# x tiles requested first on the sync queue, small parameters on the other queues, squares of tiles 1 and 3 on VectorE: a hybrid decoder block on one core

## What is computed

```python
h    = rmsnorm(x, attn_norm_w)            # x * rsqrt(mean(x*x) + eps) * w
proj = h @ w_in                           # 1024 x 3080: q, k, v, z, beta, a, conformer
qkv  = silu(causal_dwconv(proj[q,k,v], gdn_conv_w))
o    = chunked_gated_delta_rule(l2norm(q), l2norm(k), v, g, beta)   # 4 heads, chunks of 64
u    = silu(layernorm(causal_dwconv(glu(proj[cf]), cf_dw_w) + cf_dw_b, cf_ln_w, cf_ln_b))
x    = x + concat(gated_rmsnorm(o, z), u) @ w_out
x    = x + moe(rmsnorm(x, ffn_norm_w))    # top 4 of 32 experts, clamped SwiGLU
out  = rmsnorm(x, final_norm_w)
```

## Time and profile before

| | us |
|---|---|
| median of 3 runs | 1394.98 |
| lowest, highest | 1392.49, 1396.18 |
| span of the profiled execution | 1395.8 |
| first projection matmul (L1797) starts | 20.09 |
| TensorE busy | 1241.0 (89%) |
| VectorE, GpSimd, ScalarE busy | 679.5, 320.3, 223.3 |

### The profile page before, as it was taken

How to read it: one execution, slowest core, us unless ns; L and a number is a source line. 1 busy time by engine, 2 the same in 40 slices (tenths; PEclk the granted TensorE clock), 3 DMA queues, 4 the chain that set the end, 5 groups by cost and what they waited for, 6 DMA issues and landing times.

```text
span 1395.8 us, 32044 instructions
## 1 busy us (share of the span) xinstructions
PE 1241.0 (89%) x12814; PEld 585.9 (42%) x12815; DVE 679.5 (49%) x1360; ACT 223.3 (16%) x439; POOL 320.3 (23%) x432
## 2 busy tenths in 40 slices
PE   6999999999599999899899999798978887879992
PEld 3444454564235554353534445233432332335331
DVE  2898885444644364335434433345443334353428
ACT  3125543412100011000000100000110000001103
POOL 5001111000322224222223212222233222222221
PEclk9999999999799999999999999999999999999996
DMA  9212000312589999999999999999999999999996
GB/s 307 85 61 91 1 31 1 142 74 86 210 337 400 409 418 424 425 426 426 426 425 425 424 426 425 426 426 425 426 424 425 426 427 425 426 426 426 380 407 245
DMA packets 59374, 455.33 MB, mean 326 GB/s; under 512 B 13308, under 2 KB 23604, under 8 KB 34214
## 3 DMA queue, kind: packets, MB, share of 16 engines
q1 hardware_dynamic: 44262, 432.59, 74.8%
q0 software_dynamic: 11568, 18.92, 3.7%
q10 hardware_dynamic: 3504, 3.26, 0.9%
HBM read 445.02 MB, written 14.81 MB: 329 GB/s over the span
## 4 chain that ended last, share of the span: by engine, by line
PE 58%; DMA 29%; DVE 7%; issue 2%; ACT 2%; ACTq 1%; POOL 0%; SPq 0%; DVEq 0%; POOLq 0%
PE bank L2136 26%; DMA ring<-in_w_gate_up_dram 15%; PE bank L2189 14%; DMA dslots<-in_w_down_dram 14%; PE bank L1797 6%; PE bank L1987 4%; DVE dslots L1122 3%; PE bank L1792 2%; DVE hbuf L1697 1%; PE bank L1865 1%; PE bank L1872 1%; PE bank L2100 1%; PE bank L2122 1%; PE bank L1952 1%; PE bank L1956 1%
## 5 line engine op out<-in xcount | busy, mean ns | idle before, releaser
L2136 PE MATMUL bank<-ring,wq 128*32 128x512 f32 x4992 | 566.6, 601 | 64.9 <-DMA ring<-in_w_gate_up_dram 56.2
L2136 PEld LDWEIGHTS bank<-ring,wq 128*32 128x32 f32 x4992 | 208.8, 111 | 381.1 <-issue 344.3
L2189 PE MATMUL bank<-dslots,intra 128*32 128x256 f32 x5056 | 284.7, 380 | 22.6 <-DMA dslots<-in_w_down_dram 21.8
L2189 PEld LDWEIGHTS bank<-dslots,intra 128*32 128x32 f32 x5056 | 169.1, 110 | 148.3 <-issue 54.6
L1510 DVE TENSOR_REDUCE small<-bank 128x4 f32<-128x8 f32 x33 | 5.5, 166 | 409.8 <-PE bank L2100 409.8
L1007 ACT ACTIVATE zrows<-intra 128x1024 f32<-128x1024 f32 x31 | 32.8, 1059 | 790.0 <-DVE intra L1603 763.8
L1797 PE MATMUL bank<-hbuf,ring 128*128 128x512 f32 x320 | 148.5, 604 | 0.7 <-ACT hbuf L748 0.7
L616 POOL COPY idx_in<-idx 128x4 int32 (+1 forms) x32 | 11.8, 370 | 555.6 <-DVE wq L1488 534.4
L1575 DVE STREAM_TRANSPOSE wq<-bank 128x512 f32<-128x512 f32 x124 | 77.8, 685 | 71.7 <-PE bank L2136 71.7
L621 POOL DMA_INDIRECT wq<-xn_rows,idx_in x82 | 100.5, 1225 | 44.3 <-POOL idx_in L616 28.0
L626 POOL DMA_INDIRECT y_rows<-rows,idx_out x79 | 81.0, 1025 | 52.5 <-POOL idx_out L616 25.2
(11 more groups left out here) (294 smaller groups left out, 894.4 us busy)
## 6 DMA issues: line engine op xcount, KB each, us to landing
ring<-in_w_gate_up_dram SPq DMA_DIRECT2D x127, 2048.0 KB
dslots<-in_w_down_dram SPq DMA_DIRECT2D x61, 2048.0 KB
ring<-in_w_in_dram SPq DMA_DIRECT2D x12, 1024.0 KB, 13.5
ring<-in_w_out_dram SPq DMA_DIRECT2D x4, 1024.0 KB, 5.6
ring<-in_w_down_dram SPq DMA_DIRECT2D x4, 1024.0 KB
dslots<-y_rows SPq DMA_DIRECT2D x2, 2048.0 KB, 20.1
hbuf<-in_x_dram SPq DMA_DIRECT2D x4, 512.0 KB, 5.4
dslots<-in_w_down_dram SPq DMA_DIRECT2D x2, 1024.0 KB, 4.7
```

Source lines behind the costliest of these rows:

```text
L2136: ins = M(bank[g][GROUP * j:GROUP * (j + 1), :], x[:, g, c * GROUP:(c + 1) * GROUP], w[:, :, j * QD:(j + 1) * QD], start=(c == 0), stop=(c ...
L2189: ins = M(b[GROUP * j:GROUP * (j + 1), col:col + QD], actT[:, g, c * GROUP:(c + 1) * GROUP], w[:, cc, j * QD:(j + 1) * QD], start=(c == 0 ...
```

## The change

All four x tiles are requested by SyncE, ahead of everything else on its queue. The six small parameter tensors move to ScalarE's queue, behind cf_dw_w. The three gate requests move to GpSimd, behind the identity and before the masks. normcol moves on ScalarE's queue behind the four tiles. The squares of tiles 1 and 3 move to VectorE (a scalar_tensor_tensor with accumulated sum), which signals ScalarE by a new semaphore, `ssx_ready`; ScalarE keeps Ln and Exp of all tiles.

```diff
@@ block.sync
-            sp.dma_start(xr[:, 0, :], x2d[0:P, :]).then_inc(x_in[0], 16)
-            for i, v in enumerate((cf_dw_b, cf_ln_w, cf_ln_b)):
-                sp.dma_start(prow[TAPS + i:TAPS + i + 1, :], v).then_inc(param_in, 16)
-            sp.dma_start(prow[34:46, :], gdn_conv_w[0].rearrange("w (s c) -> (w s) c", s=3)).then_inc(param_in, 16)
-            sp.dma_start(prow[46:48, :], attn_norm_w.rearrange("o (r c) -> (o r) c", r=2)).then_inc(param_in, 16)
-            sp.dma_start(prow[48:50, :], ffn_norm_w.rearrange("o (r c) -> (o r) c", r=2)).then_inc(param_in, 16)
+            for t in range(T):
+                sp.dma_start(xr[:, t, :], x2d[t * P:(t + 1) * P, :]).then_inc(x_in[t], 16)
             for u in range(NU):
@@ block.gpsimd
             pool.wait_ge(consts_ready, 1)
+            pool.dma_start(wab, win[:, :, OFF_BA:OFF_BA + 2 * H]).then_inc(gate_in, 16)
+            pool.dma_start(dtb, gdn_dt_bias[0:1, :].to_broadcast([P, H])).then_inc(gate_in, 16)
+            pool.dma_start(nA, gdn_a_log[0:1, :].to_broadcast([P, H])).then_inc(gate_in, 16)
@@ block.scalar
             act.dma_start(prow[0:TAPS, :], cf_dw_w[0]).then_inc(param_in, 16)
-            for t in range(1, T):
-                act.dma_start(xr[:, t, :], x2d[t * P:(t + 1) * P, :]).then_inc(x_in[t], 16)
-            act.dma_start(wab, win[:, :, OFF_BA:OFF_BA + 2 * H]).then_inc(gate_in, 16)
-            act.dma_start(dtb, gdn_dt_bias[0:1, :].to_broadcast([P, H])).then_inc(gate_in, 16)
-            act.dma_start(nA, gdn_a_log[0:1, :].to_broadcast([P, H])).then_inc(gate_in, 16)
-            act.dma_start(normcol, gdn_norm_w.rearrange("o p -> p o")).then_inc(late_in, 16)
+            for i, v in enumerate((cf_dw_b, cf_ln_w, cf_ln_b)):
+                act.dma_start(prow[TAPS + i:TAPS + i + 1, :], v).then_inc(param_in, 16)
+            act.dma_start(prow[34:46, :], gdn_conv_w[0].rearrange("w (s c) -> (w s) c", s=3)).then_inc(param_in, 16)
+            act.dma_start(prow[46:48, :], attn_norm_w.rearrange("o (r c) -> (o r) c", r=2)).then_inc(param_in, 16)
+            act.dma_start(prow[48:50, :], ffn_norm_w.rearrange("o (r c) -> (o r) c", r=2)).then_inc(param_in, 16)
             act.wait_ge(consts_ready, 1)
             for t in range(T):
                 act.wait_ge(x_in[t], 16)
-                own.mark(A(zrows[:, (t % 2) * D:(t % 2) * D + D], xr[:, t, :], ACT.Square,
-                           accum_out=ssx[:, t:t + 1]))
-                own.settle()
+                if t % 2 == 0:
+                    own.mark(A(zrows[:, 0:D], xr[:, t, :], ACT.Square, accum_out=ssx[:, t:t + 1]))
+                    own.settle()
+                else:
+                    act.wait_ge(ssx_ready, t // 2 + 1)
                 own.mark(A(rstdx[:, t:t + 1], ssx[:, t:t + 1], ACT.Ln, bias=epst, scale=1.0 / D))
...
+            act.dma_start(normcol, gdn_norm_w.rearrange("o p -> p o")).then_inc(late_in, 16)
             act.dma_start(bgu_rows, b_gate_up[0]).then_inc(bias_in, 16)
@@ block.vector
             for t in range(T):
+                if t % 2 == 0:
+                    dve.wait_ge(x_in[t + 1], 16)
+                    V.scalar_tensor_tensor(out=zrows[:, D:2 * D], in0=xr[:, t + 1, :], scalar=1.0,
+                                           in1=xr[:, t + 1, :], op0=ALU.mult, op1=ALU.mult,
+                                           accum_out=ssx[:, t + 1:t + 2]).then_inc(ssx_ready, 1)
                 dve.wait_ge(rstdx_ready, t + 1)
```

More of the change, by code:

```diff
@@ L299, in block_kernel @@
         router_ready, rows_known = sem("router_ready"), sem("rows_known")
+        ssx_ready = sem("ssx_ready")
         norm_halved, csum_ready = sem("norm_halved"), sem("csum_ready")
```

## The result

The changed kernel takes **1399.38 us** (median of 20 runs, 1394.82 to 1401.13), and the kernel before 1396.38 (20 runs, 1392.49 to 1398.36). The ratio is **1.0021, 95% interval 1.0015 to 1.0028**: 2.1 to 3.9 us slower, 2.9 in the middle. That is inside the bound of 0.3%, and inside the range that was forecast; the forecast shift was +1.7 us. Of that, 1.4 us is the kernel before, whose median is 1396.38 over 20 runs where the forecast started from 1394.98 over three; the rest is the larger shift.

The account below looks back on a forecast made before the run. The start of the first projection matmul was taken to bound the kernel: parameters at 12.2 plus 9.6 us gives 21.8, +1.7 over 20.09. Added to the 1395.0 us median that makes 1396.7 us, range 1391.5 to 1400.2.

Parts of the forecast that it names:

- P: Landing of the last parameter for TensorE: forecast about 12.2 us against 9.2 before, bounds 6.1 and 14.7.
- the even step of one row in 0.25 us: On the DMA engine shared by cf_dw_w and x: rows alternate one for one, 25 remaining parameter rows taking 6.2 us.
- The case of P near 10: Shared DMA engine serves queues in long runs of rows: parameters near 10, first projection matmul 19.6, 1394.5 us; chance 0.07.
- F: Start of the first projection matmul on TensorE: forecast 21.8 us against 20.09 before, +1.7 us.
- ScalarE's five requests: On ScalarE's queue between tile 3's last Exp and the first eviction: five requests with normcol, 2.56 us, four before.
- Scale and transpose of tile 3 ... hide below 0.4 + 2.56: Tile 3's scale and transpose, 0.8 + 1.2 us from its square's end, were said to hide behind ScalarE's Exp and requests.
- The other edits: Gate requests on GpSimd, later normcol and ring units: costed at nothing; gate issuing bounded at 1.225 to 9.8 us for wab.
- One for one to the end: A shift of the first projection matmul was said to carry through to the kernel's end in full.
- Parameters first: Rival: parameter rows get through before later x tiles, landing at 6.1 to 9.2 us; gain 3.0 to 1.3 us; chance 0.2.
- Stuck behind the ring: Rival: parameter requests overtaken by SyncE's first ring request, landing at 14.7 us, +4.2 us or more; chance 0.15.
- Both inputs early: Rival: shared DMA engine no brake, tile 3 in by 9.5 and parameters at 6 us; 4.5 us gained; chance 0.05.
- Gate columns late: Rival: TensorE waits at L1747 for gate columns landing after 33 us, +4.2 us; chance 0.03.

Follow-up runs that it names:

- e1: Changed kernel with the 31-row cf_dw_w request made as two, of 16 and 15 rows; ratio 0.9997 against the kernel before, -0.4 us.
- e11: Kernel before, unchanged, profiled a second time; only profiled, no ratio given.
- e9: Kernel before with cf_dw_w split, gate requests on GpSimd, ScalarE's later requests behind its evictions, and filler matmuls on TensorE; ratio 0.9963, -5.2 us.
- e10: Kernel before with only the cf_dw_w request split into 16 and 15 rows; ratio 0.9975, -3.5 us.
- e2: Kernel before with only the squares of tiles 1 and 3 moved to VectorE, all requests as before; ratio 0.9995, -0.7 us.
- e3: Changed kernel with all four squares back on ScalarE, so only the requests moved; ratio 1.0012 against the kernel before, +1.7 us.
- e4: Changed kernel with the square of tile 1 ahead of the parameter work on VectorE; ratio 1.0009 against the kernel before, +1.3 us.
- e8: Kernel before with two extra squares of tile 3 on ScalarE as a plain 2.4 us delay; ratio 1.0029, +4.0 us.
- e7: Changed kernel with cf_dw_w split, tile 1's square earlier, TensorE fillers, and ScalarE's five later requests behind evictions; ratio 1.0015 against the kernel before, +2.1 us.

## Why the prediction was right, and where its working was off

**Where the parameters land (P): right in time and in mechanism, not in its even pace.** 12.2 was forecast, and 12.37 and 12.27 were the starts of the parameter transposes in the two profiles. e1 shows that the mechanism is the one named: with cf_dw_w spread, P is 9.10 and tile 3 lands 3 us earlier. But the even step of one row in 0.25 us was not what happened. ScalarE's queue moved 2 packets between 4.5 and 5.0, then 6 and 5 in the two half microseconds from 5.5, and none between 9.0 and 9.5, in the slump beside the gate requests, which the prediction had at nothing. Faster rows early and the slump late may have offset each other; no run separates them. Tile 1 came at 9.6 (8.4 in the second profile) and not at 8.1, tile 3 at 13.1 (12.5) and not at 12.1; neither was on the path. The case of P near 10 did not come.

**From P to F: 10.0 measured, 9.6 forecast, by a wrong account.** Piece by piece, measured and forecast: parameter work 1.5 and 1.4; VectorE's squares and two scales 4.0 and 4.5 (the loss of 0.4 beside GpSimd fell on the last pair of scales, 1.88 us, behind what sets F); Ln and Exp 0.4 and 0.4; ScalarE's five requests 2.8 and 2.56; a wait for TensorE 0.5 and nothing; eviction 0.74 and 0.74. The half microsecond too much on VectorE and the half missing on TensorE cancel: that part is luck. The step that failed is "Scale and transpose of tile 3 ... hide below 0.4 + 2.56". ScalarE's five requests were through at 21.12 (20.39 and 0.73 for the last), but the eviction waited until 21.61 for TensorE:

```profile
20.39 0.73 ACTq L746 DMA_DIRECT2D ffnw<-in_ffn_norm_w_dram  x1
...
21.61 2.42 ACT L750 ACTIVATE hbuf<-bank,small 128x512 f32<-128x512 f32 x4 [3.09 <-PE bank L1739]
```

The prediction costed TensorE's part by the last tile alone, at the pace of rows 3's end. It did not ask what 32 transposes take in a row once the scales come in pairs. They start behind tile 0's scale, and 24 of them at 0.214 us stand before the one that F needs. In the kernel before they had started at 13.62, with a scale every 1.6 us, and when tile 3's scale was done at 18.28, TensorE was through with the first 24. It was close even there: the chain of the second profile of the kernel before (e11) runs through 24 transposes, 4.80 us. ScalarE's limit and TensorE's lie 0.5 us apart, which is why the sum was nearly right.

**The other edits: no wait seen for the gate columns, but not nothing.** GpSimd made the gate requests in 1.12, 0.59 and 0.54 us. The masks were complete at 25.42 (21.33 before), eleven microseconds ahead of VectorE's need, and the gate columns' matmuls followed the first projection tile without a wait:

```profile
3.45 1.12 POOL L495 DMA_DIRECT2D small<-in_w_in_dram  x1 [0.31 <-POOL consts L492]
...
25.22 0.20 POOL L544 MEMSET dslots<- 128x120 f32 x1
```

1024 pieces cost 1.12 us, and 128 pieces 0.54 to 0.59, so the upper bound of 9.8 was far too wide. The prediction priced the issuing and the landing of these requests, and not what they do to the transfers beside them: the slump from 8.5 to 10 us above.

**One for one to the end: held, with noise.** Shift of F against measured time, in us: -5.5 and -5.2 (e9), -3.0 and -3.5 (e10), -1.2 and -0.4 (e1), -0.6 and -0.7 (e2), +1.0 and +1.7 (e3), +1.5 and +1.3 (e4), +2.3 and +2.9 (changed). Each lies within its interval, 0.9 to 1.9 us either way. e8 does once its slower first matmuls are counted. e7 does not (-0.9 and +2.1).

**The size.** The forecast +1.7 lies just below the interval of 2.1 to 3.9 us. F moved by 2.3 (22.35 against 20.09), or 2.0 in the mean of two profiles each (22.15 against 20.16), which lies just outside that interval. Of the missing 1.2 us, 0.4 to 0.5 are the transposes, and the rest, up to a microsecond, is not attributed. Whether later starts meet clock drops more often on average was not shown: there are two profiles of each kernel, and one of the changed kernel's has no drop at all.

**The rivals.** Parameters first: no, P was later by 3 us. Stuck behind the ring: not at 14.7, though e1 shows the mild form of it, a last small request that takes 5.3 us. Both inputs early: no. Gate columns late: no.

## What to carry to other kernels

Before a request is moved to "a free queue", look at how many DMA engines it runs on: a 31-row request ran down a single one, row by row with everything else on that engine, and held a 128-row tile's last part and, it seems through a full queue, requests that had nothing to do with it. Cutting it into 16 and 15 rows gave 3.5 us here; try that before anything is reordered. Small scattered requests have a price beside their issue: look at the GB/s of all DMA queues while they land (109 in place of 311 here). When a pacing engine is relieved, cost what it had spread out: here 32 transposes that had nearly kept pace with the squares became one run of 6.3 us, at half rate for most of it, on an engine that had done almost nothing before.

## What the runs showed of the hardware

**The first transposes ran at half pace, and the profile's clock did not tell.** In the changed kernel the 128x128 passes of the transposes followed each other at 0.214 us for some 5.2 us (4.6 in its second profile, 3.5 in the kernel before) and then at 0.109. The count of each 2 us stretch hints at it (10 from 16 to 18 us, 14 from 20 to 22), while the clock, the third number from the end, is 1.00 in both:

```profile
16.00:18.00 2.00, 2.00 (x10) 1.00 1.10 347
20.00:22.00 2.00, 2.00 (x14) 1.00 1.10 336
```

In e9, with fillers ahead, it is 20 from 11 to 13 us:

```profile
11.00:13.00 2.00, 2.00 (x20) 1.00 1.10 350
```

So the start of a program has to be read from the spacing of matmuls. That TensorE runs at half rate at first and after a pause is also in the Trainium skill ("TensorE: Matmul & The Clock Gate", Part 1: The HAM clock gate), and the trace agrees: a factor of two, at the start of the changed kernel, and gone when the engine was kept busy.

**How many engines a request uses.** 31 rows used one, 16 and 15 rows used many. The Trainium skill ("DMA: Bandwidth & Descriptors", Why a DMA increments its semaphore by 16 and not by 1) has this: the largest number up to 16 that divides the slowest dimension of both sides, so 1 for 31, 16 for 16 and 15 for 15. The rows of e1 agree as far as they go: 40.2% of sixteen engines in q10 is the time of more than six, and 8.2% in rows 6 little more than one.

**A float32 128x128 matmul with float32 operands ran as two passes**: 56 written, 112 in the trace. The transposes ran as one (32 written, 32 in the trace). A filler is to be sized by the trace and not by the count in the code.
